# Another order of loads and first products in a two-block transformer, and group norm's root, weight, bias and gate on GpSimd

## What is computed

```
kv = _rmsnorm(mem, a_mem_norm[0]) @ a_w_mem_kv[0]      # [256,1024] @ [1024,512], the kernel's first product
...
z    = rmsnorm(x, norm1_w_2[0]) @ w_in_2[0]
y    = chunkwise_retention(...)                        # [256 tokens, 8 heads, 64]
yn   = (y - mean(y)) * rsqrt(var(y) + GN_EPS)          # over the 64 of a head
o_b  = (yn * ret_gn_w_2 + ret_gn_b_2) * silu(gate)     # gate: 512 columns of z
x    = x + concat(o_a, o_b) @ w_out_2[0]               # o_a: the sparse attention
```

## Time and profile before

| | |
|---|---|
| Median of three runs | 911.14 us (911.08, 911.14, 912.14) |
| Profiled execution, its own time | 912.54 us |
| Its span, first to last instruction | 910.8 us |
| TensorE matmul busy | 900.0 us, 99% |
| VectorE, ScalarE, GpSimd busy | 608.3, 489.0 and 65.5 us |
| Mean granted TensorE clock | 0.998 |

### The profile page before, as it was taken

The page is one execution under the profiler, slowest core; times in us unless marked ns, Lnnn a source line. Parts: engine busy times, 40 slices in busy tenths (PEclk is TensorE's granted clock), DMA queues, the critical chain, the costliest instruction groups (busy, mean ns, idle before and its releaser), DMA issues.

```text
span 910.8 us, 13492 instructions
## 1 busy us (share of the span) xinstructions
PE 900.0 (99%) x4811; PEld 755.2 (83%) x4811; DVE 608.3 (67%) x927; ACT 489.0 (54%) x755; POOL 65.5 (7%) x124
## 2 busy tenths in 40 slices
PE   9999999999999999999999999999998999999998
PEld 8778788888888887768888888888886888888887
DVE  5868867555555687874755555668998666555565
ACT  7666756444444475873644444555577554444442
POOL 1311112000000010000200000012320000000000
PEclk9999999999999999999999999999999999999999
DMA  8935155655555551436755555436361446555541
GB/s 294 344 133 182 56 189 204 207 185 184 185 190 192 172 185 46 167 134 233 254 199 193 184 184 188 154 128 230 95 208 47 139 142 229 184 185 194 189 169 47
DMA packets 96884, 159.88 MB, mean 176 GB/s; under 512 B 5968, under 2 KB 37920, under 8 KB 96840
## 3 DMA queue, kind: packets, MB, share of 16 engines
q1 hardware_dynamic: 94240, 155.08, 51.1%
q10 hardware_dynamic: 2568, 4.21, 1.4%
q0 software_dynamic: 32, 0.02, 0.0%
HBM read 158.21 MB, written 3.16 MB: 177 GB/s over the span
## 4 chain that ended last, share of the span: by engine, by line
PE 94%; DVE 4%; ACT 1%; issue 1%; POOL 0%; DVEq 0%; POOLq 0%; ACTq 0%
PE turn L1754 10%; PE proj L1754 9%; PE proj L1698 6%; PE score L1698 6%; PE proj L1700 6%; PE proj L1699 6%; PE score L1699 6%; PE score L1700 6%; PE outp L1698 5%; PE outp L1700 5%; PE outp L1699 5%; PE turn L1758 5%; PE proj L1758 5%; PE turn L1744 2%; PE score L1896 1%; PE turn L1906 1%
## 5 line engine op out<-in xcount | busy, mean ns | idle before, releaser
L2027 DVE TENSOR_TENSOR wlo<-raw,whi 128x2048 fp32r<-128x2048 f32 (+1 forms) x131 | 297.2, 2278 | 167.5 <-ACT whi L1449 132.7
L1449 ACT ACTIVATE whi<-raw 128x2048 fp32r<-128x2048 f32 x64 | 122.7, 1917 | 162.6 <-PE turn L1758 76.2
L1438 ACT ACTIVATE whi<-raw 128x2048 fp32r<-128x2048 f32 (+1 forms) x67 | 126.2, 1895 | 60.7 <-PE score L1700 17.0
L1698 PE MATMUL proj<-whi,set 128*128 128x512 f32 (+2 forms) x266 | 104.9, 394 | 0.0
L1700 PE MATMUL proj<-whi,set 128*128 128x512 f32 (+2 forms) x266 | 102.2, 384 | 0.0
L1699 PE MATMUL proj<-wlo,set 128*128 128x512 f32 (+2 forms) x266 | 102.0, 383 | 0.0
L1754 PE MATMUL turn<-set,whi 128*128 128x512 f32 x384 | 96.3, 393 | 0.0
L1754 PE MATMUL proj<-set,whi 128*128 128x512 f32 x384 | 95.6, 391 | 0.0
L1698 PE MATMUL score<-whi,set 128*128 128x512 f32 x232 | 91.5, 394 | 0.0
L1699 PE MATMUL score<-wlo,set 128*128 128x512 f32 x232 | 90.6, 391 | 0.0
L1700 PE MATMUL score<-whi,set 128*128 128x512 f32 x232 | 90.4, 390 | 0.0
(11 more groups left out here) (252 smaller groups left out, 1283.9 us busy)
## 6 DMA issues: line engine op xcount, KB each, us to landing
raw<-in_a_w_up SPq DMA_DIRECT2D x32, 512.0 KB, 4.2
raw<-in_a_w_down SPq DMA_DIRECT2D x32, 512.0 KB, 4.5
raw<-in_b_w_up SPq DMA_DIRECT2D x32, 512.0 KB, 4.2
raw<-in_b_w_down SPq DMA_DIRECT2D x32, 512.0 KB, 4.6
raw<-in_w_gate SPq DMA_DIRECT2D x22, 512.0 KB, 4.0
raw<-in_w_up SPq DMA_DIRECT2D x22, 512.0 KB, 5.0
raw<-in_w_down SPq DMA_DIRECT2D x22, 512.0 KB, 3.9
raw<-in_a_w_in SPq DMA_DIRECT2D x20, 512.0 KB, 6.5
```

Source lines behind the costliest of these rows:

```text
L1438: return act.activation(shaped(whi, u)[:, ks, :], shaped(raw, u)[:, ks, :], ACT.Copy)
L1449: act.activation(shaped(whi, u), shaped(raw, u), ACT.Copy).then_inc(hi_done, 1)
L1698: pe.matmul(out_, hi, wh, start=start, stop=False)
L2027: return dve.tensor_tensor(shaped(wlo, u)[:, ks, :], shaped(raw, u)[:, ks, :], shaped(whi, u)[:, ks, :], ALU.subtract)
```

## The change

1. **The start.** `mem`'s first half is loaded in two transfers of 256 columns (256 KB each), the second of them behind unit 0's first half. Each turn_operand of that half waits for its own transfer. The norm weight `a_mem_norm` gets its own semaphore, is turned by itself right after the first filler and copied to `gcol` by itself (`turn_first_gain`, step "first_gain"); the other two follow later. The fillers become 12, 6 and 2 transposes. `first_half` becomes a step of its own ahead of turn_operand 2 and 3, waits only for the first two blocks of `mem`, and takes block 0 as soon as block 0 of the weights is split. Splits of units 0, 1 and 2 are two steps each ("split", "split_rest"), so that an operand's split can stand between.
2. **Group norm.** GpSimd takes the inverse root ("group_sum" on GpSimd, by `inverse_of_sums`); VectorE waits for it in group_scale. GpSimd does weight, bias and gate for both tiles, one after the other. VectorE's group_gain and group_gate are empty.
3. **Orders.** `MOVES` is changed for the start and for the second block's attention: on VectorE, select 12, 13 and 14 go ahead of group_scale, and exps 32 follows it; on TensorE, keep_busy 1 goes behind scores 17; on ScalarE, split 54 goes ahead of turn_weights 32. Other steps between units 99 and 107 also change places.

```diff
-WARM = (17, 21)
+PARTED = 3
+WARM = (12, 6, 2)
...
+        add("first_gain")
         m1 = [turn_mem(0)]
+        add("keep_warm").n = WARM[1]
+        add("keep_warm").n = WARM[2]
         add("first_gains")
         split(1)
+        st = add("first_half")
+        st.use, st.lhs = m1[0], 1
...
-            def load_memory(h):
-                cols = slice(h * COLS, (h + 1) * COLS)
+            def load_memory(i):
+                cols = (slice(0, TOK), slice(TOK, COLS), slice(COLS, D))[i]
...
             load_memory(0)
             load_half(0, 0)
+            load_memory(1)
             load_half(0, 1)
-            load_memory(1)
+            load_memory(2)
...
+                elif st.kind == "group_sum":
+                    inverse_of_sums(st.st, st.st.rs, st.st.va, DH, GN_EPS)
                 elif st.kind == "group_gate":
-                    y = o_nat[:, 0, 512:1024]
-                    pool.wait_ge(yn_done, 1)
                     pool.wait_ge(gn_landed, 32)
-                    behind(pool.tensor_tensor(y, y, gn[:, 0, :], ALU.mult))
-                    behind(pool.tensor_tensor(y, y, gn[:, 1, :], ALU.add))
-                    pool.wait_ge(*st.st.gate)
-                    pool.tensor_tensor(y, y, zq[:, 1, 0, :], ALU.mult).then_inc(ob_done, 1)
+                    for t in range(NT):
+                        y = o_nat[:, t, 512:1024]
+                        pool.wait_ge(yn_done, t + 1)
+                        behind(pool.tensor_tensor(y, y, gn[:, 0, :], ALU.mult))
+                        behind(pool.tensor_tensor(y, y, gn[:, 1, :], ALU.add))
+                        pool.wait_ge(*st.st.gate)
+                        pool.tensor_tensor(y, y, zq[:, 1, t, :], ALU.mult).then_inc(ob_done, 1)
...
-                pe.wait_ge(hi_half, 1)
-                for t in range(NT):
-                    for k in range(2):
+                for k in range(2):
+                    pe.wait_ge(hi_half, k + 1)
+                    for t in range(NT):
                         pe.matmul(bank[t][:], set_hi[lhs][:, k, tok(t)], wh[:, k, :], start=k == 0, stop=False)
...
+            def turn_first_gain():
+
+                pe.wait_ge(first_gain_landed, 16)
+                pe.transpose(Sb[gain_s[0] % 2][:, COLS - KT:COLS], grow[0][0:KT, :], ident[0:KT, 0:KT])\
+                  .then_inc(first_gain_turned, 1)
...
-                    behind(ins)
-                    inverse_rms(group.rs, group.va, DH, GN_EPS)
+                    ins.then_inc(sum_done, 1)
                 elif st.kind == "group_scale":
                     group = st.st
+                    wait_inverse(group)
...
-                elif st.kind == "group_gain":
-                    y = o_nat[:, 1, 512:1024]
-                    dve.wait_ge(yn_done, 2)
-                    dve.wait_ge(gn_landed, 32)
-                    behind(dve.tensor_tensor(y, y, gn[:, 0, :], ALU.mult))
-                    behind(dve.tensor_tensor(y, y, gn[:, 1, :], ALU.add))
-                elif st.kind == "group_gate":
-                    y = o_nat[:, 1, 512:1024]
-                    dve.wait_ge(*st.st.gate)
-                    dve.tensor_tensor(y, y, zq[:, 1, 1, :], ALU.mult).then_inc(ob_done, 1)
```

More of the change, by code:

```diff
@@ L385, in build @@
         landed = [sem(f"unit_landed{i}") for i in range(RING)]
-        half_landed = [[sem(f"half_landed{u}_{i}") for i in range(2)] for u in range(HALVED)]
+        half_landed = [[sem(f"half_landed{u}_{i}") for i in range(2)] for u in range(PARTED)]
+        hi_first = sem("hi_first")
+        lo_first = sem("lo_first")
         hi_half = sem("hi_half")
@@ L444, in build @@
         consts_made = sem("consts_made")
-        mem_landed = [sem(f"mem_landed{i}") for i in range(2)]
+        mem_landed = [sem(f"mem_landed{i}") for i in range(3)]
         x_landed = [sem(f"x_landed{i}") for i in range(2)]
@@ L490, in split @@
             while split_next[0] <= u:
+                n = split_next[0]
                 st = add("split")
-                st.u = split_next[0]
+                st.u, st.part = n, 0 if n < PARTED else None
+                if n < PARTED:
+                    st = add("split_rest")
+                    st.u, st.part = n, 1
                 split_next[0] += 1
@@ L1116, in build @@
         group = add("group_square")
+        inverse_use(group)
         group.o, group.va, group.rs = last[1], col(16), col(16)
@@ L1522, in _ @@
                     act.activation(st.lam[:, 2:4], st.lam[:, 0:2], ACT.Exp).then_inc(lam_exp, 1)
-                elif st.kind == "split":
-                    split_hi(st.u)
+                elif st.kind in ("split", "split_rest"):
+                    split_hi(st.u, st.part)
                 elif st.kind == "square_sum":
@@ L1839, in _ @@
                     warm_up(WARM[0])
+                elif st.kind == "first_gain":
+                    turn_first_gain()
+                elif st.kind == "first_gains":
+                    turn_gains(0)
+                elif st.kind == "keep_warm":
+                    warm_up(st.n)
                 elif st.kind == "constants":
@@ L1846, in _ @@
                     n = st.use[st.b]
-                    if st.b == 0:
+                    if isinstance(st.ready, list):
+                        wait(st.ready[st.b])
+                    elif st.b == 0:
                         wait(st.ready)
@@ L1852, in _ @@
                     turn_bank(n, lambda t, k: st.src[:, t, k * P:(k + 1) * P], [k0, k0 + 1])
-                    if n == 1:
-                        turn_gains(0)
-                        warm_up(WARM[1])
+                elif st.kind == "first_half":
+                    wait(turned(st.use - 1))
+                    first_half(st.lhs, banks["P"])
                 elif st.kind == "multiply":
@@ L1860, in _ @@
                         wait_turned(st.use)
-                    if st.u == 0 and 0 in st.tiles:
-                        first_half(st.lhs, banks[st.bank])
                     if st.u == 1:
@@ L2009, in behind, with split_lo @@
                 dve.wait_ge(dve_chain, chain[0])
-            def split_lo(u, hi=None):
+            def split_lo(u, hi=None, part=None):
                 if u >= N_UNITS:
                     return
-                if u < HALVED:
-                    for i, (made, done) in enumerate(((hi_half, lo_half), (hi_done, lo_done))):
-                        dve.wait_ge(made, u + 1)
-                        lo_blocks(u, range(2 * i, 2 * i + 2)).then_inc(done, 1)
+                if u < HALVED and part == 0:
+                    for k in range(2):
+                        dve.wait_ge(hi_half, 2 * u + k + 1)
+                        ins = lo_blocks(u, [k])
+                    ins.then_inc(lo_half, 1)
+                    return
+                if u < HALVED:
+                    dve.wait_ge(hi_done, u + 1)
+                    lo_blocks(u, range(2, UK)).then_inc(lo_done, 1)
+                    return
+                if part is not None:
+                    cs = UNITS[u].parts[part][2]
+                    made, done = ((hi_first, 1), (lo_first, 1)) if part == 0 else ((hi_done, u + 1), (lo_done, 1))
+                    dve.wait_ge(*made)
+                    dve.tensor_tensor(shaped(wlo, u)[:, :, cs], shaped(raw, u)[:, :, cs], shaped(whi, u)[:, :, cs],
+                                      ALU.subtract).then_inc(*done)
                     return
@@ L2203, in _ @@
                     dve.wait_ge(lam_done, 1)
-                elif st.kind == "split":
-                    split_lo(st.u)
+                elif st.kind in ("split", "split_rest"):
+                    split_lo(st.u, part=st.part)
                 elif st.kind == "turn_operand":
```

49 lines of the change are left out of this document (35 added, 14 removed), and 173 rows, old and new, of the table MOVES.

## The result

The changed kernel is slower. Its median is 913.90 us (22 runs, 911.88 to 915.73) against 912.33 for the kernel before in the same set of runs (22 runs, 911.08 to 913.88). The ratio is 1.0021, with a 95% interval of 1.0015 to 1.0027: about 1.9 us. In a second set of runs it was 1.0032 (1.0021 to 1.0042). The forecast of 908.7 us was wrong in sign, and 913.90 lies outside its range. Of the 5.2 us between the two, 1.2 is the kernel before itself, whose median was 912.33 here and 911.14 when the forecast was made; the other 4.0 are the gain of 2.45 that was forecast and the difference of 1.57 between the two medians the other way.

The account below looks back on a forecast made before the run. TensorE, busy 900.0 of 910.8 us, was taken as the bound. Gains of 1.5 (start) and 0.95 (group norm) made 2.45, giving 908.35 on the span and 908.7 off the 911.14 median; range 906.9 to 911.2.

Parts of the forecast that it names:

- The start: Opening loads and first products: multiply 0 begins at 11.3 instead of 13.05 us; 1.5 us gained, bounds 0.4 to 1.9.
- The rest as now: Loads at the start: after mem's smaller first transfers, all other loads land as before.
- My bound of 0.4: Smallest gain at the start, if mem's first 256 KB landed only at 5.2 and the rest slipped 0.3.
- The tightest later unit is unit 4: Loads after the start: unit 4 has 2.0 us of slack against the 1.5 gained, so the gain survives.
- From 55 us on the weights are waiting: After the start: from 55 us weights are already loaded and each engine follows TensorE.
- the start is swallowed: Rival: late first transfer or unit 4 leaves 0.4 to 0.6 us of the start's gain; 910.9 or 909.9; chance 0.13.
- The orders of 560 to 665: Reordered steps, 628 to 665 us in the prediction: no effect, within 0.4 us either way.
- TensorE fully busy: Reason given for no effect from the reordered steps of 628 to 665 us, within 0.4 either way.
- The middle: Group norm and second block's attention: multiply 72 starts at 692.2 instead of 693.15; 0.95 us gained, bounds +0.5 to -2.5.
- GpSimd's root 2.1 us, hidden: Group norm: the root's six GpSimd instructions take 2.1 us, 674.8 to 676.9, behind three VectorE select rounds of 2.8.
- the six: GpSimd's weight, bias and gate for both tiles: 1.13 to 1.29 each alone, starting at 679.5, done at 687.9.
- The rival of the wrong sign: Rival "slower": GpSimd and VectorE block each other, six instructions at 2.62 each, 915.9 us; chance 0.07.

Follow-up runs that it names:

- e1: The changed start alone, with group norm and the later orders set back, against the kernel before: ratio 1.0005 (0.9996 to 1.0013), +0.5 us.
- e9: The kernel before with only weight, bias and gate of both tiles on GpSimd and the changed orders from scores 16 on: ratio 1.0000 to the kernel before.
- e3: The changed start alone, with unit 4's load issued ahead of the small constants, against the kernel before: ratio 1.0020 (1.0007 to 1.0033).
- e10: The changed kernel with mem's first half in one transfer, old orders of 560 to 665 us, root on VectorE: ratio 0.9989 to the kernel before.

## Why the prediction was wrong

**The start, forecast -1.5, won nothing: about +0.35, with the sign open.** In the profiled execution the steps on TensorE, ScalarE and VectorE up to 12 us were right within 0.3 us; in the six other traces with two transfers TensorE waited 0.31 to 2.34 us for the second one. Two steps failed.

- "The rest as now". I priced the transfers one by one and took the stream behind them as unchanged. Around the two transfers of 256 KB the queue moved 196 to 275 GB/s in 4 to 6 us, where it moved 337 to 372 with one, and what was queued behind them was later. ScalarE began unit 4's split, right when it landed, at 29.0 to 30.3 in the eight traces with one transfer and the constants in front, and at 29.7 to 31.8 in the six with two. My bound of 0.4 allowed for a late first landing, not for a slower stream, so it didn't contain a loss.
- "The tightest later unit is unit 4", with 2.0 us of slack. Unit 4's first matmul indeed came almost without a wait (about 0.1), at 34.49. But behind unit 4 VectorE works off four low splits and the rotation of the queries in a row, and the splits are fed by loads. Before, the rotation ended at 46.0 and TensorE came at 46.63 for it: 0.66 us of slack. "From 55 us on the weights are waiting" was true and beside the point, since the lead was gone at 47. The rival "the start is swallowed", with a chance of 0.13, comes nearest; it still kept 0.4 to 0.6.

**The orders of 560 to 665, forecast 0 within 0.4, came to +0.55.** "TensorE fully busy" is no cover: a full engine has no slack to take up a wait, and ScalarE's copy came 0.33 late.

**The middle, forecast -0.95 with +0.5 as its worst, won nothing and most likely lost about 1.0**: 86.17 against an estimated 85.0 at full clock, and in the two profiled executions, both with the lowered clock, 87.49 against 86.52 from 655 to 741 us. Against e1's trace (86.06) it would be 0.1. What failed first is the step "GpSimd's root 2.1 us, hidden". I took the power's 0.69 from rows of 2 columns for a tile of 16; it took 2.91 in each of the five traces that have it, and the root 4.4 us. I had a row of 2.62, read it as VectorE's interference and made it 0.6 late. For that row the reading was right: it lies at 147.09 us, beside VectorE's low splits of 2048 columns. The 2.91 had only instructions of 0.43 us and less beside it. What it cost: group_scale began at 679.84, and with the root back on VectorE the wait at turn_operand 27 goes from 1.60 to 0.33 or nothing. The rest held: the six took 1.26 to 1.58 each, 8.45 us with gaps (forecast 8.4), and the stall before scores 17 was 1.26 (forecast about 1). By the factor of two in the Trainium skill's "GPSIMD Engine Reference", section 4.1 (Engine selection), the six would, as an estimate, have been done at 689.0. They were at 689.13, but because they began 1.2 us late. That page's warning was right in its result all the same: with the root on VectorE the six on GpSimd won nothing (e9, +0.4 at full clock).

What failed second is the base of that term. I made it against the profiled execution, which had the lowered clock in 680 to 690, and took it off a median of executions that by their times (911.08, 911.14) had none. The 2.07 us of stall was one draw as well: the second trace of the kernel before has 1.21. So a part of what I wanted to remove was probably not in the number that I took it from; how large a part, the runs don't show.

**The rival of the wrong sign wasn't it.** It had all six near 2.62, and none of them went above 1.60; the one long instruction was the power. The loss came from three terms that I had as a gain, a gain and nothing. (The forecast's lower end, 906.9, also takes 2.3 for the middle where its bound was 2.5.)

**The sum**: 0.35, 0.55 and 1.0 make 1.9 us; 1.9 was measured (1.4 to 2.5), and 2.9 in the second set. That they meet so well is partly luck: by the executions at 1.00 the start would be 1.0, which leaves 0.1 for the middle of the 1.6 measured there. Shown are that the start's 1.5 and the middle's 0.95 didn't come, where each was lost, and the size of the orders' 0.55. Open are the sign of the start (e1's interval is -0.4 to +1.2), the size of the middle (0.1 to 1.2), why the second set lies 1 us higher, and how often an execution meets the lowered clock. That share differs between kernels (9 of 12 in e3, 3 of 12 in e10) and, for the kernel before, between sets (14 of 28, 6 of 24), and no part here explains it.

## What to carry to other kernels

When a start is fed by loads, ask of each new transfer what it does to the rate of all that are queued behind it, and follow the lead through every chain that hangs on a load to a step with real slack, not only to the next unit. Price a moved instruction by a row of its own width on the engine that it moves to; if there is none, let the range run to the cost in proportion to the width. Before a gain is taken off a median, see whether the executions behind that median have the stall or the lowered clock that the profiled one shows; a second profile of the same kernel showed 1.21 us of stall here instead of 2.07.

## What I had not expected of the hardware

- GpSimd's power of two tensors takes 0.69 to 0.72 us for 128x2 in most rows, and 2.91 for 128x16 in all five traces that have one, while its other instructions on the same 16 columns take 0.20 to 0.22. Beside VectorE's low splits of 2048 columns a power of 128x2 has also taken 2.62 to 2.84. VectorE's root on the same 16 columns takes 0.17 to 0.18 us for each of its twelve instructions.
- Where VectorE and GpSimd each started a 128x512 instruction with two inputs within 0.06 us, the first took its usual time (0.69 on VectorE in one trace, 1.29 on GpSimd in the other) and the second took 1.79 and 1.77.
- With the same instructions, the mean granted clock is 1.00 in 63 of 109 executions of the kernel before and lower in the others. In both profiled ones the clock falls towards the 1.2 GHz level behind the stall in 680 to 695 us. That it is there in the unprofiled ones too is inferred; between the medians at 1.00 and at 0.998 lie 1.8 us (911.2 and 913.0).
